# The norms at the turn to the second attention: roots by Sqrt and a correction on VectorE instead of pow on GpSimd, and tile 1 transposed inside v's first tile

## What is computed

```python
def rms_norm_2(x, g):
    y = x * lax.rsqrt(jnp.mean(x * x, axis=-1, keepdims=True) + EPS)     # EPS = 1e-6
    return y * g

y = gmlp_mixer(rms_norm_2(h, a_pre_g), a_w_in, ln_g, ln_b, w_s, b_s, a_w_out)
h = h + rms_norm_2(y, a_post_g)            # norm "a"
kv_in = rms_norm_2(h, kv_norm_g)           # norm "h3": the rows' factor is shared
k = kv_in @ w_k                            #   by this norm ...
v = kv_in @ w_v
q, z = split(rms_norm_2(h, b_pre_g) @ b_w_in)   # ... and by this one
out = swa_mixer_core(q, k, v, sinks)
h = h + rms_norm_2((out * silu(z)) @ b_w_out, b_post_g)
```

## Time and profile before

| | us |
|---|---|
| median of 3 runs | 885.76 (885.38 to 886.71) |
| the profiled execution, its own time | 885.75 |
| span of its trace | 884.0 |
| TensorE busy | 868.2 (98% of the span) |
| VectorE, ScalarE, GpSimd busy | 537.2, 360.3, 542.8 |
| granted TensorE clock | 1.00 in every stretch named below |

### The profile page before, as it was taken

The page is one execution under the profiler, slowest core; times in us unless marked ns, Lnnn a source line. Parts: engine busy times, 40 slices in busy tenths (PEclk is TensorE's granted clock), DMA queues, the critical chain, the costliest instruction groups (busy, mean ns, idle before and its releaser), DMA issues.

```text
span 884.0 us, 11936 instructions
## 1 busy us (share of the span) xinstructions
PE 868.2 (98%) x4220; PEld 722.0 (82%) x4220; DVE 537.2 (61%) x880; ACT 360.3 (41%) x804; POOL 542.8 (61%) x604
## 2 busy tenths in 40 slices
PE   8999999999999999999999999999997999999997
PEld 6888888888888787888888888888887888888886
DVE  6125648875035489775765535556996457788624
ACT  4123333431134377546112321113775536767622
POOL 7766556587789832317975038771359798566352
PEclk9999999999999999999999999999999999999999
DMA  7533231342322468885742253526962222112202
GB/s 198 167 120 96 74 92 51 96 143 92 128 90 96 124 146 177 208 203 190 162 124 95 73 190 96 125 90 152 217 180 71 72 73 93 51 49 72 73 1 95
DMA packets 81517, 102.65 MB, mean 116 GB/s; under 512 B 11826, under 2 KB 54322, under 8 KB 81459
## 3 DMA queue, kind: packets, MB, share of 16 engines
q1 hardware_dynamic: 72752, 85.12, 30.1%
q0 software_dynamic: 8704, 16.78, 11.2%
q10 hardware_dynamic: 2, 0.00, 0.0%
HBM read 99.79 MB, written 2.10 MB: 115 GB/s over the span
## 4 chain that ended last, share of the span: by engine, by line
PE 88%; POOL 4%; DVE 2%; DMA 2%; ACT 2%; issue 1%; POOLq 0%; DVEq 0%; ACTq 0%
PE bank L2076 26%; PE bank L2078 26%; PE bank L2077 26%; PE bank L2319 2%; PE bank L2347 1%; PE bank L2173 1%; DMA gain<-in_a_w_in 1%; DVE wlo L1667 1%; POOL wlo L850 1%; PE bank L2292 1%; PE bank L2342 1%; PE bank L2341 1%; DMA raw<-in_a_w_in 1%; POOL ms L795 1%; POOL whi L841 1%
## 5 line engine op out<-in xcount | busy, mean ns | idle before, releaser
L850 POOL TENSOR_TENSOR wlo<-raw,whi 128x512 fp32r<-128x512 f32 x204 | 280.4, 1404 | 0.7 <-ACT whi L972 0.7
L841 POOL TENSOR_SCALAR whi<-raw 128x512 fp32r<-128x512 f32 x202 | 140.8, 733 | 188.1 <-PE bank L2078 179.1
L2076 PE MATMUL bank<-actB_hi,whi 128*128 128x512 f32 (+1 forms) x416 | 159.6, 384 | 0.6 <-POOL wlo L850 0.6
L2077 PE MATMUL bank<-actB_lo,whi 128*128 128x512 f32 (+1 forms) x416 | 158.7, 381 | 0.0
L2078 PE MATMUL bank<-actB_hi,wlo 128*128 128x512 f32 (+1 forms) x416 | 158.5, 381 | 0.0
L2076 PE MATMUL bank<-whi,actA_hi 128*128 128x512 f32 x318 | 125.9, 396 | 1.2 <-DVE actA_lo L1421 0.7
L2078 PE MATMUL bank<-whi,actA_lo 128*128 128x512 f32 x318 | 124.0, 390 | 0.0
L2077 PE MATMUL bank<-wlo,actA_hi 128*128 128x512 f32 x318 | 123.9, 390 | 0.0
L2076 PEld LDWEIGHTS bank<-actB_hi,whi 128*128 128x128 f32 x416 | 78.3, 188 | 15.4 <-issue 1.1
L2078 PEld LDWEIGHTS bank<-actB_hi,wlo 128*128 128x128 f32 x416 | 78.2, 188 | 15.2
L2077 PEld LDWEIGHTS bank<-actB_lo,whi 128*128 128x128 f32 x416 | 78.3, 188 | 14.1
(11 more groups left out here) (269 smaller groups left out, 1579.4 us busy)
## 6 DMA issues: line engine op xcount, KB each, us to landing
raw<-in_a_w_in SPq DMA_DIRECT2D x44, 512.0 KB, 4.2
raw<-in_w_in SPq DMA_DIRECT2D x32, 512.0 KB, 3.9
raw<-in_b_w_in SPq DMA_DIRECT2D x16, 512.0 KB, 3.4
raw<-in_a_w_out SPq DMA_DIRECT2D x12, 512.0 KB, 3.3
gain<-in_a_w_out POOLq DMA_DIRECT2D x9, 512.0 KB, 8.2
raw<-in_w_out SPq DMA_DIRECT2D x8, 512.0 KB, 3.4
raw<-in_w_ple_gate SPq DMA_DIRECT2D x8, 512.0 KB, 3.3
gain<-in_a_w_in POOLq DMA_DIRECT2D x8, 512.0 KB, 7.7
```

The source lines that it names most:

```text
L841: pool.tensor_scalar(H, src[:, i * HALF:(i + 1) * HALF], 1.0, 1.0, ALU.mult, ALU.mult).then_inc(w_hi, 1)
L850: ins = pool.tensor_tensor(L, src[:, i * HALF:(i + 1) * HALF], H.bitcast(f32), ALU.subtract)
L2076: M(out_, whi_, xhi_, start=start, stop=False)
L2077: M(out_, whi_, xlo_, start=False, stop=False)
```

## The change

It does five things.

- The roots of norms a and h3 leave GpSimd. The squares are scaled by 1/64 instead of 1/32, so sums are a quarter of the mean square. ScalarE adds EPS/4 to one half's sum (`add_eps`, Identity with a bias), and `std` takes Sqrt(other half's sum + that), which is half of the root. VectorE then does `inverse`: four instructions of 128x1, sum x = last + ms; 1/root; x * (1/root) + root, which is a Newton step for the square root; reciprocal, which is rstd.
- ScalarE needs the table of Sqrt: one more ACT_TABLE_LOAD and a dummy Sqrt behind `square_a(1, 0)`, ahead of `hi_a(10)`.
- For tile 1 the second half's square of h is made by VectorE (`square_v`, two SBUF operands), and `std("h3", 1)` takes it as its bias.
- Tile 1 is transposed inside v5 of tile 0: block `v5h 0` is the first half of that product and waits for one `actB_lo` piece only; `v5 0` is the second half. `normed_n` is two instructions of 128x512.
- On GpSimd all eight roots of a and h3 are gone, and one wait is new: `wlo` of k5's first half waits for the third `h3_ready`, that is for the first half of tile 1 of h.

At the start a memset of 128x1 is added on GpSimd, and VectorE's memset of `gcv` moves behind three others.

```diff
-    o += turn("n", 0) + turn("n", 1) + [("v5", 0), ("v5", 1)]
+    o += turn("n", 0) + [("v5h", 0)] + turn("n", 1) + [("v5", 0), ("v5", 1)]
...
-            after[at("v5", 0, 1) - 0.25] = [lambda: root("a", 0, D), lambda: root("a", 1, D)]
-            after[at("v5", 0, 1)] = [lambda: root("h3", 0, D)]
-            after[at("k5", 0, 0) - 0.5] = [lambda: root("h3", 1, D)]
...
+            after[at("k5", 0, 0) - 0.5] = [lambda: pool.wait_ge(h3_ready, 3)]
...
+            def std(name, t, c, done):
...
+                if (name, t) in BY_V:
+                    act.wait_ge(v_squared, BY_V[name, t])
+                else:
+                    act.wait_ge(std_step, STD_STEP["eps", name, t // 2 * 2 if name == "a" else t])
+                act.wait_ge(squared[name], done)
+                A(rstd[:, n, t:t + 1], ss[:, n, t, c:c + 1], ACT.Sqrt, bias=ms[:, n, t:t + 1]).then_inc(std_step, 1)
...
+            act.wait_ge(consts_made, 6)
+            A(lams[:, 7:8], eps[:, 0:1], ACT.Sqrt)
...
             scale_two("k5", 1)
             h3_out(0)
-            h3_out(1)
+            h3_square(1, 0)
             normed_n(0)
+            turned("n", 0, 0)
+            std("h3", 1, 0, 3)
+            turned("n", 0, 1)
             normed_n(1)
-            turned_n(0)
             square_a(2, 0)
+            std("a", 2, 0, 7)
             turned_n(1)
...
+            def inverse(name, t):
...
+                dve.wait_ge(std_step, STD_STEP[name, t])
+                V.tensor_scalar(mean, last, ms[:, n, t:t + 1], None, ALU.add).then_inc(root_step, 1)
+                V.reciprocal(first, root).then_inc(root_step, 1)
+                dve.wait_ge(root_step, nth + 2)
+                V.tensor_scalar(sum_, mean, first, root, ALU.mult, ALU.add).then_inc(root_step, 1)
+                dve.wait_ge(root_step, nth + 3)
+                V.reciprocal(root, sum_).then_inc(rstd_ready[name], 1)
...
             lo_a(13, (0,))
             part_gain(0, 1)
+            inverse("a", 0)
             lo_a(13, (1,))
+            h3_in(0)
             part_gain(1, 1)
-            h3_in(0)
-            h3_in(1)
+            inverse("a", 1)
+            h3_in(1, (0,))
+            inverse("h3", 0)
+            h3_in(1, (1,))
+            square_v(1)
             add_kept(6, 0, p03_kept(0), a_out_(2, 0), (c7_made, 28 + 6))
+            rest("n", 0, 0)
+            inverse("h3", 1)
+            rest("n", 0, 1)
             add_kept(6, 1, p03_kept(1), a_out_(3, 0), (c7_made, 28 + 10))
-            rest_n(0)
             part_gain(2, 0)
             rest_n(1)
+            inverse("a", 2)
             h3_in(2)
             part_gain(3, 0)
-            h3_in(3)
+            inverse("a", 3)
+            h3_in(3, (0,))
+            inverse("h3", 2)
+            h3_in(3, (1,))
+            inverse("h3", 3)
```

More of the change, by code:

```diff
@@ L153 @@
 LANDED = landings()
+STD_STEP = {step: n + 1 for n, step in enumerate(
+    [("eps", "a", 0), ("eps", "a", 2), ("a", 0), ("a", 1), ("eps", "h3", 0), ("h3", 0), ("h3", 1),
+     ("a", 2), ("a", 3), ("eps", "h3", 2), ("h3", 2), ("eps", "h3", 3), ("h3", 3)])}
+ROOTED_LAST = {("a", t): int(t < 2) for t in range(4)} | {("h3", t): int(t != 1) for t in range(4)}
+BY_V = {("x", 0): 1, ("x", 1): 2, ("h3", 1): 3}
+H3_SQUARES = [(0, 0), (0, 1), (1, 0), (2, 0), (2, 1), (3, 0), (3, 1)]
 SQUARES_A = [(0, 0), (1, 0), (2, 1), (3, 1), (0, 1), (1, 1), (2, 0), (3, 0)]
@@ L802, in root_attn @@
                 pool.tensor_scalar(ms_attn[:, h, :], ss_attn[:, h, :], 1.0 / DV1, SUBLN_EPS, ALU.mult, ALU.add)\
-                    .then_inc(msq_attn, 1)
-                pool.wait_ge(msq_attn, h + 1)
+                    .then_inc(ms_ready, 1)
+                pool.wait_ge(ms_ready, next(roots))
                 pool.tensor_tensor(r_attn[:, h, :], ms_attn[:, h, :], mhalf[:, 0:1].to_broadcast([P, T]), ALU.pow)\
@@ L1234, in square_a, with add_eps, h3_square @@
                 square("a", t, c, a_out_(t, c))
+            def add_eps(name, t, tiles, c, done):
+                n = NORMS[name]
+                act.wait_ge(squared[name], done)
+                A(ms[:, n, t:t + tiles], ss[:, n, t:t + tiles, c], ACT.Identity, bias=eps[:, 0:1]).then_inc(std_step, 1)
+            def std(name, t, c, done):
+                n = NORMS[name]
+                if (name, t) in BY_V:
+                    act.wait_ge(v_squared, BY_V[name, t])
+                else:
+                    act.wait_ge(std_step, STD_STEP["eps", name, t // 2 * 2 if name == "a" else t])
+                act.wait_ge(squared[name], done)
+                A(rstd[:, n, t:t + 1], ss[:, n, t, c:c + 1], ACT.Sqrt, bias=ms[:, n, t:t + 1]).then_inc(std_step, 1)
+            def h3_square(t, c):
+                act.wait_ge(h3_ready, 2 * t + c + 1)
+                square("h3", t, c, resid[:, t, c * HALF:(c + 1) * HALF])
             def h3_out(t):
-                for c in range(2):
-                    act.wait_ge(h3_ready, 2 * t + c + 1)
-                    square("h3", t, c, resid[:, t, c * HALF:(c + 1) * HALF])
+                h3_square(t, 0)
+                add_eps("h3", t, 1, 0, H3_SQUARES.index((t, 0)) + 1)
+                h3_square(t, 1)
+                std("h3", t, 1, H3_SQUARES.index((t, 1)) + 1)
             def y4_hi(j):
@@ L1303, in normed_n @@
                 act.wait_ge(rstd_ready["h3"], t + 1)
-                A(n_place(t), resid[:, t].rearrange("p (a b) -> p a b", a=2), ACT.Copy,
-                  scale=rstd[:, NORMS["h3"], t:t + 1]).then_inc(tok_ready["n"], 1)
+                for j in range(2):
+                    A(n_place(t)[:, j], resid[:, t, j * HALF:(j + 1) * HALF], ACT.Copy,
+                      scale=rstd[:, NORMS["h3"], t:t + 1]).then_inc(tok_ready["n"], 1)
             def scale_two(s, h):
@@ L1443, in _ @@
             V.memset(base1[0:64, HALF - 64:HALF], MASKED).then_inc(base_step, 1)
+            V.memset(gcv[:, :, 0:2], 0.0).then_inc(base_step, 1)
             def square_x(t):
@@ L1896, in part_gain, with h3_in @@
                     .then_inc(a_gained, 1)
-            def h3_in(t):
+            def h3_in(t, halves=(0, 1)):
                 dve.wait_ge(rstd_ready["a"], t + 1)
                 dve.wait_ge(a_gained, 4 + t + 1)
-                for c in range(2):
+                for c in halves:
                     half = slice(c * HALF, (c + 1) * HALF)
@@ L1904, in h3_in, with square_v @@
                                            resid[:, t, half], ALU.mult, ALU.add).then_inc(h3_ready, 1)
+            inverses = count(0)
+            def inverse(name, t):
+                n, c = NORMS[name], ROOTED_LAST[name, t]
+                nth = 3 * next(inverses)
+                last, mean, first, sum_ = (ss[:, n, t, k:k + 1] for k in (c, 1 - c, 2, 3))
+                root = rstd[:, n, t:t + 1]
+                dve.wait_ge(std_step, STD_STEP[name, t])
[5 more added lines that the diff above has]
+                V.reciprocal(root, sum_).then_inc(rstd_ready[name], 1)
+            def square_v(t):
+                dve.wait_ge(h3_ready, 2 * t + 2)
+                half = resid[:, t, HALF:D]
+                V.tensor_tensor_reduce(acc[:, 0, :], half, half, 1.0 / (4 * D), EPS / 4, ALU.mult, ALU.add,
+                                       ms[:, NORMS["h3"], t:t + 1]).then_inc(v_squared, 1)
             def rest_n(t):
@@ L2224, in ready @@
                     pe.wait_ge(lo["p"], 2)
-                if kind == "v5":
-                    pe.wait_ge(lo["n"], 2 * (s + 1))
+                if kind in ("v5h", "v5"):
+                    pe.wait_ge(lo["n"], 2 * s + (2 if b == ("v5", 0) else 1))
                 if kind == "sc":
@@ L2326, in work @@
                     rows = slice(t * P, (t + 1) * P)
-                    for k in range(KD):
+                    for k in range(0 if kind == "v5h" or t else KD // 2, KD // 2 if kind == "v5h" else KD):
+                        if k == 4:
+                            pe.wait_ge(lo["n"], 2 * t + 2)
                         H, L = halves_of(n, k // 2)
```

49 lines of the change are left out of this document (30 added, 19 removed).

## The result

The changed kernel takes **889.33 us** (median of 6 runs, 888.32 to 890.53) against 885.75 us (6 runs, 885.30 to 886.71) for the kernel before, run on the same chip: a ratio of 1.0042, with a 95% interval of 1.0029 to 1.0054. That is 3.6 us slower. It lies inside the predicted range (883.0 to 889.6) but 2.1 us above the forecast of 887.2, and on the side that the forecast had given a third of the chance: by the bound of 0.2% it is slower, not the same.

What follows compares the result with a forecast made beforehand. TensorE, busy in nearly all of the span, was taken as the bound, with 5.41 us idle to win; the held layout ended at 695.3 against 693.84, +1.5 on 885.75, so 887.2 us, range 883.0 to 889.6.

Steps and rivals of the forecast that it cites:

- The layout up to v5: Instruction times laid out from 658.1 us: TensorE's first turn at 668.3, 0.15 earlier; v5 starts at 671.7, before 672.09.
- The gain of tile 0: VectorE ahead of the first turn: held by GpSimd's second v5 subtraction, some 1.8 us instead of 0.68, ending at 661.5.
- the wait inside unit 13: TensorE ahead of the first turn: a new wait of 0.6 us, as VectorE's second `wlo` ends at 663.2.
- the square: VectorE's square of tile 1: queues behind GpSimd's second k5 subtraction, some 1.7 us long, ending at 670.4.
- GpSimd scales q5: GpSimd goes straight from k5 to q5 at 674 instead of 680.82, holding VectorE's `h3_in` and gain.
- The table load: ScalarE ahead of `hi_a(10)`: 1.28 us, with the dummy Sqrt some 1.5, beside 2.00 idle; costs nothing.
- 2.9 idle us ahead of T2: TensorE before tile 2's turn: 2.9 us idle where 1.25 was, turning at 684.5 instead of 682.15.
- The root's term: VectorE's four small instructions at 0.15 us: 0.6 from Sqrt to rstd, 8 times, 4.9 us more.
- small steps queue: Rival: each `inverse`'s first and third step waits behind GpSimd's `wlo` or `whi`; +5.6 us, 891.3; chance 0.08.
- the variant with the first step alone: Small-step case on VectorE: only the first step of each `inverse` is held by GpSimd; +3.1 us, 888.9.
- fewer collisions: Rival: k5's subtractions or q5's work miss VectorE's; -0.7 us each, towards -3.6 together, 882.2 to 885.3; chance 0.27.
- the gain of tile 3: VectorE around tile 2's turn: held by GpSimd's q5 work, ending at 681.25.

Runs made afterwards that it cites:

- The run with one reciprocal: Changed kernel with k5's first-half subtractions after tile 1's square and each root one VectorE reciprocal instead of four instructions, correcting step left out: 881.70 us, ratio 0.9950.
- the one wait: Changed kernel with GpSimd's subtractions of k5's first half waiting for VectorE's square of tile 1, not the first half of its h: 885.10 us, ratio 0.9999.
- the fill: Changed kernel plus unread small TensorE products, 8 ahead of v5's first half and 12 ahead of tile 2's turn: 887.61 us, ratio 1.0022.
- the run with GpSimd's work cut: Changed kernel with GpSimd's scaling, rounding and subtractions of k5's first half and q5's first two units cut to 16 columns each: 882.64 us, ratio 0.9966.
- the one with the old order and the wait for the square: Changed kernel with k5's first-half subtractions after tile 1's square and both tiles turned before v5's first half: 885.73 us, ratio 1.0000.

## Why the prediction came out as it did

**The layout up to v5 was right.** With the 1.5 us of 347 us taken off, T0 stands at 668.3 (forecast 668.3) and V0 at 671.6 (671.7). The gain of tile 0 took 1.78 (1.8), the wait inside unit 13 was 0.55 (0.6), the square 1.64 (1.7), and GpSimd scales q5 from 673.9 (674). The table load of 1.28 at ScalarE stood beside idle time, and `hi_a(10)` behind it still waited 0.49 for TensorE: cost nothing, as said.

**The step that failed is the clock.** The prediction had 2.9 idle us ahead of T2, and over 2 between the first turn (668.3, some 1 us long) and V0 (671.7), and priced each idle stretch at its own length. The sum has no term for the clock: all products behind the idle stretches are priced as before, where the column says 1.00 everywhere in the turn and no gap there is over 1.72. v5 of two tiles ended 1.1 us later than forecast (679.8 against 678.7), which the wait ahead of T2 swallowed, and from T2 to T3 the kernel took 5.37 instead of the forecast 3.9, which nothing swallowed. Filling the gaps gave back 1.7 us, so with the clock at 1.00 the kernel takes 887.6: **0.4 us from the forecast.** The range had room for 889.33 because of rivals that are all about holds; that it also covers the half clock, which none of them names, is luck.

**The root's term was mis-sized.** From Sqrt's end to rstd I had 0.6 for four small instructions at 0.15. The four lines of the changed kernel (min/median/max in ns):

```profile
L1960 DVE TENSOR_SCALAR ss<-ss,ms x8: 198/203/214, 662.5 to 688.1; 128x1 f32<-128x1 f32 x8
...
L1961 DVE RECIPROCAL ss<-rstd x8: 147/148/155, 662.6 to 688.2; 128x1 f32<-128x1 f32 x8
...
L1963 DVE TENSOR_SCALAR ss<-ss,rstd x8: 272/273/277, 662.8 to 688.4; 128x1 f32<-128x1 f32 x8
...
L1965 DVE RECIPROCAL rstd<-ss x8: 164/165/165, 663.1 to 688.7; 128x1 f32<-128x1 f32 x8
```

The step with two per-partition operands takes 0.27, and from first start to last end a root takes 0.78. Laid out again with these numbers the end moves by 1.2 us; in the trace T2 is 0.6 later than forecast. The row that I used had constants as operands, which was the nearest one and not the same form. The run with one reciprocal puts the three further steps, 0.63 us at each root, at 3.4 us together: T2 alone came 2.2 earlier. That is more than my layout gave them (2.7).

**The rival "small steps queue" is refuted.** Its condition was that the first and third step stand behind GpSimd's `wlo`. They were never held: the longest of eight is 0.214 and 0.277, though some lie right inside a `wlo`, as these of VectorE and GpSimd do:

```profile
672.95 0.20 DVE L1960 TENSOR_SCALAR ss<-ss,ms 128x1 f32<-128x1 f32 x1
673.07 0.15 DVE L1961 RECIPROCAL ss<-rstd 128x1 f32<-128x1 f32 x1
673.25 0.27 DVE L1963 TENSOR_SCALAR ss<-ss,rstd 128x1 f32<-128x1 f32 x1
```

```profile
672.84 2.51 POOL L863 TENSOR_TENSOR wlo<-tok,whi 128x512 fp32r<-128x512 f32 x2
```

So the sentence of the Trainium skill (SBUF — State Buffer, Who interferes with whom) on tensor_scalar and the mode with two ports doesn't bite for one column. That section of the Trainium skill lets tensor_scalar contend only where its operands meet the conditions of that mode, and the prediction read it without them. The rival's time, 891.3, was 2 us off, and that the measured 889.33 stands near the variant with the first step alone (888.9) is no support for it.

**The rival "fewer collisions" had the right lever.** Without k5's subtractions between the halves and the square my layout gave 0.7 us less than before; the run gave 885.10 against 885.65, the same within the noise (ratio 0.9999). The changed kernel didn't go that way because the release by the third half of h puts these subtractions exactly there. Before, they stood behind the root of tile 1, which waits for its squares: **the roots on GpSimd had also kept GpSimd's long instructions out of the way.** The prediction saw the hold and laid it out with the right length, and its two layouts, +1.5 with it and -0.7 without, put it at 2.2 us, where the medians at the full clock say 2.5. What it gave too little weight is that the clock comes on top: without the hold there is no long gap either. In one place its holds were too many: the gain of tile 3 took 0.68 in the trace and was not held.

**What stays open.** The 3.6 us don't divide into exact sums: the one wait gives 4.2 with its clock, which is the whole loss, the fill 1.7, and the prices of the roots and holds depend on each other and on whether the clock falls. Nor did any run show where 0.7 us of the run with GpSimd's work cut come from, or the 0.7 by which the single reciprocal gave more than its layout.

## What to carry to other kernels

Price an idle stretch of TensorE by its length only while it stays within what the trace shows to be harmless; beyond that add what the work behind it costs at the half clock, and see whether a later wait swallows it. When work is moved off an engine, look at what the moved instructions kept back by their waits, and put that wait back on purpose. A small instruction is priced by a row with the same kinds of operands, and a chain of roots by how many stand one behind the other.

## What the runs showed of the hardware

- TensorE's granted clock fell to 0.50 with idle stretches of 2.05, 2.06, 2.25, 2.34 and 3.56 us, and stayed at 1.00 behind those of 1.40, 1.72, 1.75 and 1.82 (the last two at 347 us, in the changed kernel and in the one with the old order and the wait for the square). It fell 0.8 us into the idle stretch in one trace and 1.9 in another of the same work, and 0.3 us behind the end of the one of 2.34. It stayed low for 3.4 us three times and for 6.8 twice (the gaps of 2.06 and 3.56).
- Products that nobody reads (128x128 against ident, 0.23 us each, two passes in the record) kept it at 1.00, and that was worth 1.7 us.
- With its columns cut to 16, a pair of GpSimd's `wlo` takes 0.40 us, and 1.40 where it meets VectorE's half of h and square (at 667.23), which themselves stay at 0.75 and 0.69. So a short instruction, too, waited 1.0 us for its turn.
